# Heads of a recurrent encoder layer: transposes, key scaling, decayed rows, the bonus and two row scalings change their places in the slot order

## What is computed

```python
def wkv_step(S, inp):
    r_t, w_t, k_t, v_t, a_t, b_t = inp
    sa = jnp.einsum('bhvk,bhk->bhv', S, a_t)
    S = S * w_t[:, :, None, :] + sa[..., None] * b_t[:, :, None, :] + v_t[..., None] * k_t[:, :, None, :]
    y = jnp.einsum('bhvk,bhk->bhv', S, r_t)
    return S, y
...
    kk = heads(k * k_k)
    kk = kk / jnp.maximum(jnp.sqrt(jnp.sum(kk * kk, axis=-1, keepdims=True)), 1e-12)
    k = k * (1 + (a - 1) * k_a)
...
    ys = layer_norm(ys, lnx_g.reshape(N_HEADS, HEAD_DIM), lnx_b.reshape(N_HEADS, HEAD_DIM), LNX_EPS)
    ys = ys + jnp.sum(rh * kh * r_k.astype(jnp.float32), axis=-1, keepdims=True) * vh
```

## Time and profile before

| | |
|---|---|
| median of 3 runs | 2696.34 us (2696.0 to 2701.8) |
| the profiled execution | 2696.08 us, of which the span is 2694.3 us |
| PE busy | 2547.0 us, 95% of the span |
| DVE, ACT, POOL busy | 1685.1, 932.5 and 1586.1 us |
| mean granted clock of PE | 0.981 of full |

### The profile page before, as it was taken

How to read it: one execution, slowest core, us unless ns; L and a number is a source line. 1 busy time by engine, 2 the same in 40 slices (tenths; PEclk the granted TensorE clock), 3 DMA queues, 4 the chain that set the end, 5 groups by cost and what they waited for, 6 DMA issues and landing times. The chain is left out here.

```text
span 2694.3 us, 65806 instructions
## 1 busy us (share of the span) xinstructions
PE 2547.0 (95%) x27280; PEld 2455.0 (91%) x27280; DVE 1685.1 (63%) x2492; ACT 932.5 (35%) x1942; POOL 1586.1 (59%) x1303
## 2 busy tenths in 40 slices
PE   8999999978888999999999999998888899999997
PEld 8999999967777999999999999988777789999996
DVE  6876328656654789931598971576555548899124
ACT  3444013444531345410245530244354214454002
POOL 6556665734324677666767766666334257776665
PEclk9999999999998999999999999999999979999998
DMA  4222232100001232223322222321000112322332
GB/s 152 95 103 85 87 99 79 63 3 5 4 20 34 86 102 99 89 87 94 93 96 95 102 82 86 100 74 41 4 4 5 35 41 94 102 95 84 88 91 77
DMA packets 81898, 193.65 MB, mean 72 GB/s; under 512 B 13680, under 2 KB 14064, under 8 KB 81648
## 3 DMA queue, kind: packets, MB, share of 16 engines
q1 hardware_dynamic: 78192, 187.07, 21.5%
q10 hardware_dynamic: 3456, 3.02, 0.4%
HBM read 186.95 MB, written 3.12 MB: 71 GB/s over the span
## 5 line engine op out<-in xcount | busy, mean ns | idle before, releaser
L850 PE MATMUL ps<-xa,w_hi 128*128 128x272 f32 x2208 | 583.3, 289 | 4.0 <-DVE w_lo L1744 2.4
L850 PE MATMUL ps<-xa,w_lo 128*128 128x272 f32 x1932 | 560.6, 290 | 0.0
L642 POOL TENSOR_SCALAR w_hi<-w_raw 128x1024 fp32r<-128x1024 f32 (+2 forms) x225 | 244.2, 1085 | 405.3 <-PE ps L736 397.5
L850 PE MATMUL ps<-xb,w_hi 128*128 128x272 f32 x1656 | 478.8, 289 | 0.0
L850 PEld LDWEIGHTS ps<-xa,w_hi 128*128 128x128 f32 x2208 | 399.1, 189 | 6.1 <-DVE w_lo L1744 2.8
L646 POOL TENSOR_TENSOR w_lo<-w_raw,w_hi 128x640 fp32r<-128x640 f32 (+2 forms) x225 | 365.5, 1624 | 0.0
L850 PEld LDWEIGHTS ps<-xa,w_lo 128*128 128x128 f32 x1932 | 364.2, 189 | 0.0
L850 PEld LDWEIGHTS ps<-xb,w_hi 128*128 128x128 f32 x1656 | 312.7, 189 | 0.0
L736 PE MATMUL ps<-hh,w_hi 128*128 128x272 f32 x1472 | 305.0, 288 | 5.6 <-DVE hl L1772 5.4
L736 PE MATMUL ps<-hh,w_lo 128*128 128x272 f32 x1472 | 302.7, 288 | 0.0
L736 PE MATMUL ps<-hl,w_hi 128*128 128x272 f32 x1472 | 302.3, 287 | 0.0
(11 more groups left out here) (351 smaller groups left out, 5667.4 us busy)
## 6 DMA issues: line engine op xcount, KB each, us to landing
w_raw<-in_wz SPq DMA_DIRECT2D x44, 512.0 KB, 3.2
w_odd<-in_w1i SPq DMA_DIRECT2D x72, 256.0 KB, 2.9
w_odd<-in_w2i SPq DMA_DIRECT2D x72, 256.0 KB, 2.9
w_raw<-in_w1i SPq DMA_DIRECT2D x68, 256.0 KB, 2.8
w_raw<-in_w2i SPq DMA_DIRECT2D x64, 256.0 KB, 2.8
w_raw<-in_w1o SPq DMA_DIRECT2D x32, 448.0 KB, 3.3
w_raw<-in_w2o SPq DMA_DIRECT2D x32, 448.0 KB, 3.3
w_raw<-in_w2i SPq DMA_DIRECT2D x20, 512.0 KB, 3.2
```

Of the source, the lines that this page charges most:

```text
L642: pool.tensor_scalar(w_hi[k][:, 0:nk, :], w_raw[k][:, 0:nk, :], 1.0, 0.0, ALU.mult, ALU.add).then_inc(w_hi_done, 1)
L850: mm = pe.matmul(ps[:, bank(site, b, j), 0:HT], w, x, start=(j in FRESH and k + i == 0), stop=(k == 3 and i == 2), skip_group_check=True)
```

## The change

Five things move, and nothing is added or removed.

- PE, `half_a` with a group of its own and one of the pair before: tiles 0 and 1 are turned ahead of steps G32 and Y of group 1, not behind them.
- PE, `half_b`: tile 2 is turned ahead of step G32 of group 0, and tiles 3 and 4 ahead of step Y.
- DVE (and the other engines' tables): `ar` of the next pair is made in slot 8 of `half_b`, not 9, and the bonus in slot 0, not 1.
- ACT: the scaling and squaring of the keys, now `keys`, goes for `p` + 1 from 2 on to the start of slot 0 of `half_a`, ahead of the copies of the turned tiles.
- ACT: the two `scaled` rows go from behind the last slot of `half_b` into slot 2.

```diff
-        IN_B = {0: (0,), 1: (1,), 3: (6,), 9: (8, 9)}
+        IN_B = {0: (0, 1), 3: (6,), 8: (8, 9)}
...
             def half_a(l, p, left, right, nxt):
                 n = l * NPAIR + p
                 for k in range(SLOTS_A):
-                    if right and k < 5:
+                    turned = left and k < 2
+                    if right and k < 5 and not turned:
                         step(7 + k, 1, n - 1)
...
                     elif left:
                         step(k - 3, 0, n)
+                    if right and turned:
+                        step(7 + k, 1, n - 1)
...
             def half_b(l, p, nxt, norm_before):
                 n = l * NPAIR + p
                 for k in range(SLOTS_B):
-                    if k < 5:
-                        step(7 + k, 0, n)
-                    elif k < 9:
-                        chunk_in(k - 5, l, p)
                     if k == 0:
                         token_major(2, n, [])
                     elif k == 1:
                         token_major(3, n, [])
                         token_major(4, n, [])
+                    if k < 5:
+                        step(7 + k, 0, n)
+                    elif k < 9:
+                        chunk_in(k - 5, l, p)
...
+            def keys(l, p, first):
+                n = l * NPAIR + p
+                if first:
+                    act.wait_ge(zs_ready, l * NSH + (7 if p == 0 else NSH + 2))
+                act.wait_ge(ar_ready, n * 3)
+                act.wait_ge(bk_ready, n * 3)
+                if not first:
+                    act.wait_ge(po_ready, n - 2)
+                act.wait_ge(rk_mm, n)
+                act.activation(kkb[:, :], row(zs, p + 6), ACT.Identity, scale=col(l, p + COL["k_k"])).then_inc(kk_ready, 1)
+                act.wait_ge(kk_ready, n + 1)
+                act.activation(tA[:, :], kkb[:, :], ACT.Square).then_inc(kksq_ready, 1)
+
             def prepare_1(l, p, k, first):
                 n = l * NPAIR + p
...
+                if k == 1 and p < 2:
+                    keys(l, p, first)
...
+                    if nxt and right and k == 0:
+                        keys(l, p + 1, False)
...
                         act.wait_ge(y_mm, n * 5)
                         act.activation(rp[:, :], ar[:, 1, 256:T], ACT.Copy).then_inc(rp_ready, 1)
+                        if 0 < p < 5:
+                            for m in range(2 * p - 2, 2 * p):
+                                scaled(l * 3, m, t_ready, l * 24 + m + 1)
...
-                if 0 < p < 5:
-                    for m in range(2 * p - 2, 2 * p):
-                        scaled(l * 3, m, t_ready, l * 24 + m + 1)
```

More of the change, by code:

```diff
@@ L1156, in half_b @@
                         token_major(4, n, [])
+                    if k < 5:
+                        step(7 + k, 0, n)
+                    elif k < 9:
+                        chunk_in(k - 5, l, p)
+                    if k < 2:
+                        pass
                     elif k == 2:
```

## The result

The changed kernel took 2679.89 us (median of 6 runs, 2670.64 to 2682.03) beside 2694.98 us of the kernel before in the same comparison (6 runs, 2688.46 to 2701.8): a ratio of 0.9932, 95% interval 0.9917 to 0.9947. The forecast of 2683.8 has the right sign, and the measured median lies in its range of 2677 to 2691, but 0.1 us under the 2680 to 2688 of its main case. As a ratio the forecast is 0.9953: outside the first interval, inside the second. The gain was forecast too small. The profiled execution took 2678.78 us at the same mean clock of 0.981, 17.3 us less than the one before.

A forecast was written before the change was run, and what follows sets the result against it. The chain from PE to DVE (sometimes ACT) and back, with each list's order, was taken to set the 47.54 us turn. Terms 8.4 + 1.0 + 4.7 - 1.6 = 12.5 us off gave 2683.8 us, range 2677 to 2691.

The forecast's parts named there:

- main case: Whole kernel: the forecast with its own range of 2680 to 2688 us, clock included; chance 0.66.
- Passage into half_a: From `half_b` to `half_a`: Y, E64 and L1030 start earlier, gaining 1.05 us in each of eight passages, 8.4 us.
- E64: PE step after Y: forecast 0.64 us earlier at the start of `half_a`, 0.8 us later in pair 0's `half_b`.
- The sign that did not come: In the changed trace, L999's wait for `ar`, 14.9 us before, would be gone or nearly so.
- Why ACT is in time: In `half_a`: keys scaled early in slot 0 let ACT's sigmoids depend on L1030 alone and end about 636.7.
- Start of half_b: Early bonus lets L1075 start without a gap: 0.48 us in pairs 1 to 4, 0.44 in pair 5, 4.7 us.
- Into pair 5: No next pair, so no L1030: passage gains only Y's 0.5 us, twice; `half_b` start there gains 0.44.
- Pair 0: Start of `half_b` without a norm to cover Y's add: E64 later, a loss of 0.8 us, twice, -1.6.
- The clock: Rival: shifted timetable meets fewer or more 1.2 GHz stretches, 3.9 us either way, 2680 to 2688; no separate chance.
- Waits that change place in `half_b`: Rival: Y has no cover in any pair, twelve starts lose 0.8 us each, 2696; chance of nothing left 0.11.
- Late sigmoids: Rival: ACT's sigmoids stay late, 0.26 to 0.4 us per eight passages not gained, 2687; chance 0.18, shared with half-gained `half_b`.
- `ar` meets POOL: Rival: in slot 8 POOL stretches `ar`, X3's add 2.4 us later in ten passages, 2708; chance 0.05.

The follow-up runs named there:

- act_back: The changed kernel with ACT's list as before (keys in slot 1 for all pairs, scaled rows behind the last slot of `half_b`): ratio 0.9948 to the kernel before.
- half_a_part: The changed kernel with `half_b` as before (tiles 2, 3 and 4 behind G32 and Y, bonus in slot 1): ratio 0.9974 to the kernel before.
- half_b_part: The kernel before with only the new `half_b` start (tiles 2, 3 and 4 ahead of G32 and Y, bonus in slot 0): ratio 0.9991.
- pair0_old: The changed kernel with `half_b`'s old tile order where no norm of a pair before runs (pair 0): ratio 0.9934 to the kernel before.
- ar_alone: The kernel before with only `ar` of the next pair moved from slot 9 to slot 8 of `half_b`: ratio 0.9964.
- table_only: The kernel before with only the new line of `IN_B` (bonus in slot 0, `ar` in slot 8): ratio 0.9957.
- ar_late: The changed kernel with `ar` back in slot 9, behind the add of X3, tiles still ahead of G32 and Y: ratio 1.0064 to the kernel before.

## Why the prediction was right in kind and too small

The mechanism was right. What failed is the size of the gain per turn, forecast as 1.53 us and measured as 1.70, and of the gain into pair 5, 0.94 against 1.13. The term mis-sized most in the sum is the start of `half_b`: 0.48 forecast, 0.57 measured alone.

- **Passage into half_a, priced 1.05.** Mechanism right at each step: X3's add late by 0.18 (it follows the start of slot 8's state update by 1.77 us, 1.59 before; 0.14 was forecast), then 1.39, 2.34, no wait for sigmoids. Measured alone: 1.10. L1030's second half comes 1.59 after E64 and not 1.96, since its matmuls begin among the last of products: counted from X3's add it is 1.60 earlier, and so 1.42 in the turn, where 1.07 was forecast. That the passage still came out near its price is because little of this reaches OUT: the scan follows DVE's masks, as forecast. G32 to OUT (at 640.68) is 9.43, 10.70 before, and 1.27 less the 0.18 is the 1.10.
- **The sign that did not come.** L999's wait for `ar` was to be gone or nearly so; 8.5 of 14.9 us are left. It was no sign of a lost gain, as this wait now lies inside that for the add of X3.
- **Why ACT is in time.** The prediction gave the credit to the early keys. `act_back` shows that the early tiles suffice. The step was not wrong in its time, but incomplete.
- **Start of half_b, priced 0.48: the term that was mis-sized most.** It measured 0.57 alone and 0.60 from head sum to E64. The 0.48 counted the waits only. PE's rows are shorter in the new order too: the head sum is followed after 0.99 us by a tile, where Y followed after 1.09, and Y after 1.07 by L1075, where a tile followed after 1.12.
- **Into pair 5, priced 0.5 + 0.44.** The last turn went from 43.60 to 42.47: 1.13. `half_a_part` has 42.91 there, 0.69, and `half_b_part` 43.17, 0.43. The 0.5 left out that E64 is 0.1 earlier still.
- **Pair 0, priced -0.8:** -0.83 in layer 0, from G32 to the next X3. That the numbers meet is luck in part. The 0.8 was meant for E64, which came 0.61 later (5.03 after G32, 4.42 before). The rest is mostly the late X3 that the early `ar` costs: `pair0_old`, with E64 back in its place, still has the next X3 0.15 later than the kernel before.
- **Sum.** 14.2 us of structure where the prediction had 12.5: 8 x 0.17 and 2 x 0.19, less 2 x 0.03. That is the part of the miss that is shown.
- **The clock.** It was held apart as a rival that shifts by up to 3.9 us. On average it gave and took nothing that these runs resolve: changed and before have 96.8 and 95.7 us at 1.2 GHz, the difference with a standard error of 3.0. In the one pair of traces 3.1 of the 17.3 us are not structure, though both have the same time at 1.2 GHz (102.5 and 102.6 us). It fell at other places: three head turns of the changed trace are longer by it by 7.1 us in all, three of the one before by 4.0, and the end of layer 0's heads is 6.35 shorter. Over all runs the mean gain is 1.7 us over the sum of the table's line. The standard error of the changed kernel's mean is 1.2 us, so this last difference is not resolved and its cause stays open. Waits filled with transposes bought no clock on average; that is what the Trainium skill, TensorE: Matmul & The Clock Gate, Part 4, would have, and these means agree with it without proving it.
- **Rivals.** Waits that change place in `half_b`: not so, E64 waits in pair 0 alone. Late sigmoids: not in the changed kernel's turns; `ar_alone` and `table_only` still have them. `ar` meets POOL: no meeting, so its price in slot 8 stays untested.

The traces do hold such meetings in stage z, which no run varied. DVE and then POOL there, in the kernel before:

```profile
521.25 1.89 DVE L2013 TENSOR_TENSOR ar<-zs,Pb 128x544 f32<-128x544 f32 x1
523.06 0.72 DVE L2019 SCALAR_TENSOR_TENSOR ar<-kkb,Pb 128x544 f32<-128x544 f32 x1
523.81 1.23 DVE L2022 TENSOR_SCALAR ar<-kkb 128x9 f32<-128x9 f32 x1
```
```profile
520.71 1.85 POOL L570 TENSOR_TENSOR nt<-kkb,aa 128x544 f32<-128x544 f32 x1
523.28 1.72 POOL L575 TENSOR_TENSOR bt<-nt,Pi 128x544 f32<-128x544 f32 x1 [0.73 <-DVE ar L2013]
```

The first and third instruction on `ar` start inside a row of POOL and are long, 1.89 and 1.23 us where they took 0.71 and 0.17 alone; the second starts ahead of L575 and takes its usual 0.72. The three are 2.24 us longer here, near the rival's 2.4, though not by the two instructions that it named. The rule of the Trainium skill, SBUF — State Buffer, section Who interferes with whom, that one fully blocks the other, agrees with the 1.89, which ends 0.58 after L570: a coincidence of rows, not a test.

Why the slow stretches fall in the same pairs of both layers in `half_b_part` and `ar_late`, and move freely in the changed kernel, stays open (two traces of the changed kernel, one of each of the others).

## What to carry to other kernels

Before an instruction is moved ahead in an in-order list, move its producer: the same tile ahead of G32 gains with `ar` one slot early and costs some 2.0 us a turn without, and 3.3 to 6.7 with the time at the lower clock that came with it. Where two engines hold each other up, two edits may each remove the same wait, and only a kernel with each left out in turn shows which is spare. Judge the structure of small edits by the length of one repeated turn at full clock, and report the time at the lower clock beside it: the runs of the kernel before span 1.0% of the whole time (2686.7 to 2713.0 us).

## What was not expected of the hardware

A wait of PE of 2.39 us came with a fall of the granted clock from 2.4 to 1.2 GHz in every turn of `ar_late` (at 635.6 us in the one shown, with PE idle since 633.7), and the time at the lower clock averaged 131.2 us there against 95.7. A microsecond at the lower clock goes with only 0.37 of a microsecond of span, where work bound by PE's clock alone would lose half: in a head turn, 6.8 us of it cost 2.39.
